# Last stage of an encoder step: the residual goes in with the first expert's result, the last expert's rows are added by 0/1 products

## What is computed

```python
lg = (xn @ w_router_group); grp = argmax(lg); top_v, top_i = top_k(le_sel, 2)
combine = sum(one_hot(eidx, 32) * wk[..., None], axis=1)
for e in range(32):
    h = silu(xn @ w_gate[e]) * (xn @ w_up[e])
    y = y + combine[:, e:e+1] * (h @ w_down[e])
x = x + y                                   # the residual
return rmsnorm(x, g_final), states, history
```

## Time and profile before

| | us |
|---|---|
| median of 3 runs | 883.58 (881.55 to 886.76) |
| the profiled execution, its own time | 883.38 |
| its span | 881.8 |
| PE busy | 792.7 (90%) |
| DVE / ACT / POOL busy | 257.7 / 118.8 / 128.3 |
| HBM read / written | 246.44 MB / 14.58 MB |

### The profile page before, as it was taken

One profiled execution on the slowest core, in us unless ns is written; L12 is line 12 of the kernel. 1 busy time (PEld: TensorE's weight loads), 2 busy tenths in 40 slices (PEclk: granted clock), 3 DMA queues, 4 the chain that ended last, 5 costly groups with the idle time before them and its releaser, 6 DMA issues.

```text
span 881.8 us, 9472 instructions
## 1 busy us (share of the span) xinstructions
PE 792.7 (90%) x3800; PEld 445.2 (50%) x3801; DVE 257.7 (29%) x730; ACT 118.8 (13%) x224; POOL 128.3 (15%) x224
## 2 busy tenths in 40 slices
PE   4999999999999999989999779779778877979876
PEld 4888888788888655533333323333223332323222
DVE  4799787100021355551111011111101111111115
ACT  5110021210100233301000000000000000000013
POOL 3000028900132200000111010000101000000000
PEclk9999999999999999999999998889899999989999
DMA  9657034062200492568999999999999999999966
GB/s 285 172 161 133 1 116 130 16 222 96 95 1 1 190 428 103 189 267 341 424 428 426 427 426 426 428 427 426 428 426 425 426 429 426 426 422 406 415 252 247
DMA packets 49056, 253.82 MB, mean 288 GB/s; under 512 B 17637, under 2 KB 18489, under 8 KB 36434
## 3 DMA queue, kind: packets, MB, share of 16 engines
q1 hardware_dynamic: 42050, 239.80, 68.1%
q0 software_dynamic: 6672, 12.86, 4.1%
q10 hardware_dynamic: 288, 0.53, 0.3%
HBM read 246.44 MB, written 14.58 MB: 296 GB/s over the span
## 4 chain that ended last, share of the span: by engine, by line
PE 63%; DMA 29%; SPq 4%; DVE 1%; issue 1%; ACT 1%; POOL 0%; POOLq 0%; ACTq 0%; DVEq 0%
PE ps L1436 26%; DMA arena<-in_w_exp_up 26%; PE ps L1688 14%; PE ps L1703 7%; PE ps L1561 6%; SPq L446 3%; PE ps L1775 2%; DMA x_rows<-arena 1%; PE ps L1500 1%; PE ps L1495 1%; DMA arena<-in_x_prompt 1%; PE ps L1678 1%; PE ps L1407 1%; PE ps L1695 1%; PE ps L1550 1%
## 5 line engine op out<-in xcount | busy, mean ns | idle before, releaser
L1688 PE MATMUL ps<-arena 128*64 128x512 f32 x1024 | 249.2, 641 | 59.2 <-DMA arena<-in_w_exp_up 58.7
L1436 PE MATMUL ps<-arena 128*128 128x272 f32 x992 | 229.6, 393 | 0.0
L1436 PEld LDWEIGHTS ps<-arena 128*128 128x128 f32 x992 | 188.1, 190 | 38.5
L1688 PEld LDWEIGHTS ps<-arena 128*64 128x64 f32 x1024 | 83.0, 148 | 203.2 <-issue 195.1
L1703 PE MATMUL ps<-arena 128*64 128x512 f32 x512 | 116.5, 595 | 2.0 <-DVE arena L1334 2.0
L1338 DVE TENSOR_SCALAR arena<-ps,arena 128x512 f32<-128x512 f32 x32 | 24.0, 751 | 201.3 <-PE ps L1703 201.3
L819 DVE TENSOR_TENSOR arena<-arena 128x256 f32<-128x256 f32 (+11 forms) x217 | 74.6, 344 | 13.3 <-ACT arena L728 4.0
L1703 PEld LDWEIGHTS ps<-arena 128*64 128x64 f32 x512 | 37.8, 137 | 65.0 <-issue 60.8
L1303 DVE TENSOR_TENSOR arena<-ps,arena 128x1024 f32<-128x1024 f32 x15 | 18.4, 1225 | 177.6 <-PE ps L1678 177.6
L588 POOL DMA_INDIRECT y_parts<-arena x32 | 32.0, 1000 | 239.9 <-DVE arena L1338 239.9
L769 ACT ACTIVATE arena<-ps,arena 128x512 f32<-128x512 f32 x32 | 22.0, 689 | 309.9 <-PE ps L1688 309.9
(11 more groups left out here) (224 smaller groups left out, 489.2 us busy)
## 6 DMA issues: line engine op xcount, KB each, us to landing
arena<-in_w_exp_gate SPq DMA_DIRECT2D x29, 2048.0 KB, 42.5
arena<-in_w_exp_up SPq DMA_DIRECT2D x29, 2048.0 KB, 32.2
arena<-in_w_exp_down SPq DMA_DIRECT2D x29, 2048.0 KB, 37.8
arena<-in_w_in SPq DMA_DIRECT2D x6, 2048.0 KB, 9.4
arena<-in_w_exp_gate SPq DMA_DIRECT2D x12, 512.0 KB, 13.2
arena<-in_w_exp_up SPq DMA_DIRECT2D x12, 512.0 KB, 18.8
arena<-in_w_exp_down SPq DMA_DIRECT2D x6, 1024.0 KB, 18.8
arena<-in_x_prompt SPq DMA_DIRECT2D x8, 512.0 KB, 6.4
```

Of the source, the lines that this page charges most:

```text
L1436: last = pe.matmul(dst[:, hh, 0:HALF], w[:, k, m * P:(m + 1) * P], rhs[:, k, hh * HALF:(hh + 1) * HALF], start=(k == 0), stop=(k == kk - 1))
L1688: last = pe.matmul(ps[n * TILE:(n + 1) * TILE, 2 + par, :], x_t[:, k, :], w[:, k, :], start=(k == 0), stop=(k == KD - 1))
```

## The change

- The residual is added with the first choice's result. DVE finds for each slot whether it is the token's first choice (`first`). ACT copies the x2 rows of a pair out of `xg`, times `first`, into `y_sb[0]` (even expert) and `x_odd` (odd expert): `fold_two`, four ACT instructions of 64x512 for a pair. `result` becomes a scalar_tensor_tensor that scales and adds.
- `xg` is still one buffer and now has a second reader, so `next_gather(j)` also waits for `folded >= 2 * j`. `fold_two(j)` stands on ACT behind the silu of expert 2j.
- `gu_rows` becomes one buffer (the other is `x_odd`), and the copy of gate and up waits for `gu_turned >= e`.
- The last expert's rows are not scattered. They are added by a product of `picks` (is this the slot's token, 0 or 1, 128 x 544, made by POOL's iota and one DVE instruction) with `y_sb[1]`. The reload of `y_parts` then waits for experts 0 to 30 alone.
- As the last expert's rows of `y_parts` are no longer written, all of `y_parts` (4.5 MB) is set to zero by 9 DMAs of POOL behind the first arrival of w_in.
- x2 is not reloaded. g_final comes as one row of 4 KB (`g_row`), and PE spreads it over the partitions with two products behind `turn_gate_up(30)`, where it waits for it.
- The last stage goes through the tiles in the order 0, 1, 2, 3, sample; the sample tile also goes through PE, with POOL adding its two parts, and DVE adds the parts of tiles 1 and 2. The mean and EPS move into the ACT instructions.

```diff
-END_ORDER = (4, 0, 1, 2, 3)
+LOAD_ORDER = (4, 0, 1, 2, 3)
+END_ORDER = (0, 1, 2, 3, 4)
...
-            sp.wait_ge(x2_stored, 16 * TT)
             sp.wait_ge(down_done, NE - 3)
-            sp.dma_start(ring[9]..., x2_rows[0:SEQ]...).then_inc(x2_back, 16)
-            sp.dma_start(x2_end[4][0:DEC], x2_rows[SEQ:NT]).then_inc(x2_back, 16)
-            sp.dma_start(g_end, a["g_final"]....to_broadcast((P, D))).then_inc(g_in, 16)
+            sp.dma_start(g_row, a["g_final"].rearrange("(o d) -> o d", o=1)).then_inc(g_in, 16)
...
             sp.wait_ge(y_all, 1)
-            for par in range(2):
-                sp.wait_ge(y_stored[par], 16 * NP)
+            sp.wait_ge(y_stored[0], 16 * NP)
+            sp.wait_ge(y_stored[1], 16 * (NP - 1))
...
+            pool.wait_ge(w_stream[0], 16)
+            by_part = y_parts.rearrange("(p n) c -> p (n c)", p=P)
+            for c in range(0, span, D):
+                pool.dma_start(by_part[:, c:c + w], zeros[:, 0:w]).then_inc(parts_zeroed, 16)
...
+            def next_gather(j):
+                pool.wait_ge(xt_done, j + 1)
+                pool.wait_ge(folded, 2 * j)
+                gather(j)
             gather(0)
-            pool.wait_ge(xt_done, 2)
-            gather(1)
+            next_gather(1)
             for e in range(NE):
-                j = e // 2 + 2
-                if e % 2 == 0 and j < NP:
-                    pool.wait_ge(xt_done, j + 1)
-                    gather(j)
+                if e >= 2 and e % 2 == 0 and e // 2 + 1 < NP:
+                    next_gather(e // 2 + 1)
+                if e == NE - 1:
+                    break
...
+            def fold(dst, rows, col, n):
+                for half in range(2):
+                    last = act.activation(dst[half * TILE:(half + 1) * TILE], xg[rows, half * F:(half + 1) * F],
+                                          ACT.Copy, scale=col[rows])
+                last.then_inc(folded, n)
+            def fold_two(j):
+                act.wait_ge(xg_in[j % 2], 16 * (j // 2 + 1))
+                if j:
+                    act.wait_ge(y_stored[0], 16 * j)
+                fold(y_sb[0], slice(0, TILE), first[:, 2 * j:2 * j + 1], 1)
+                if j:
+                    act.wait_ge(x_odd_free, j)
+                fold(x_odd, slice(TILE, P), first[:, 2 * j + 1:2 * j + 2], 1)
+            act.wait_ge(first_ready, 1)
+            fold_two(0)
...
                 gate(e % 2, e + 1)
+                if e and e % 2 == 0:
+                    fold_two(e // 2)
+                if e == NE - 2:
+                    act.wait_ge(g_spread, 1)
+                    act.activation(g_end..., ps[:, 0:2, :], ACT.Copy).then_inc(g_ready, 1)
...
-                dve.tensor_scalar(y_sb[par], ps[:, 6 + par, :], scale, None, ALU.mult).then_inc(y_ready, 1)
+                dve.wait_ge(folded, done)
+                last = dve.scalar_tensor_tensor(out=y_sb[par], in0=ps[:, 6 + par, :], scalar=scale, in1=residual,
+                                                op0=ALU.mult, op1=ALU.add)
...
+                if e == NE - 2:
+                    pe.wait_ge(g_in, 32)
+                    for half in range(2):
+                        last = pe.matmul(ps[:, half, :], ones[0:1, :], g_row[:, half * F:(half + 1) * F], start=True, stop=True)
+                    last.then_inc(g_spread, 1)
...
+            def pick(i, first, end):
+                for half in range(2):
+                    last = pe.matmul(ps[:r, 2 * (i % 4) + half, :], picks[rows, i * P:i * P + r], y_sb[1][rows, :],
+                                     start=first, stop=end)
+            pe.wait_ge(y_back[0], 16)
+            add(0, y_end[0][:, 0:D], True, False)
+            add(0, y_end[0][:, D:2 * D], False, False)
+            pe.wait_ge(y_ready, NE)
+            pick(0, False, True).then_inc(sum_done, 1)
+            for i in (1, 2):
+                pick(i, True, False)
+                pe.wait_ge(pair_sum, i)
+                add(i, y_end[i][:, 0:D], False, True).then_inc(sum_done, 1)
+            pick(3, True, False)
+            add(3, y_end[3][:, 0:D], False, False)
+            add(3, y_end[3][:, D:2 * D], False, True).then_inc(sum_done, 1)
+            pe.wait_ge(final_ready, 1)
+            pick(4, True, False)
+            pe.wait_ge(sample_sum, 1)
+            add(4, y_end[4][:, 0:D], False, True).then_inc(sum_done, 1)
```

More of the change, by code:

```diff
@@ L592, in put_entries @@
             def put_entries():
-                for par in range(2):
-                    pool.wait_ge(y_stored[par], 16 * NP)
+                pool.wait_ge(y_stored[0], 16 * NP)
+                pool.wait_ge(y_stored[1], 16 * (NP - 1))
+                pool.wait_ge(y_ready, NE)
                 pool.sem_inc(ov_done, 1)
@@ L774, in gate @@
                 act.activation(h[par], src[:, :, 0:TILE], ACT.Silu).then_inc(silu_ready, 1)
+            def fold(dst, rows, col, n):
+                for half in range(2):
+                    last = act.activation(dst[half * TILE:(half + 1) * TILE], xg[rows, half * F:(half + 1) * F], ACT.Copy,
+                                          scale=col[rows])
+                last.then_inc(folded, n)
[9 more added lines that the diff above has]
+            fold_two(0)
             act.wait_ge(slot_w_ready, 1)
             for e in range(NE):
-                if e >= 2:
-                    act.wait_ge(gu_turned, e - 1)
+                if e:
+                    act.wait_ge(gu_turned, e)
                 gate_up_out(e % 2, e + 1, slot_w[:, 1, e:e + 1])
@@ L787, in more @@
                 act.wait_ge(ov_idx, n)
+                act.wait_ge(ov_x, n * 16)
+                act.wait_ge(ov_first_ready, n)
+                fold(y_sb[0], slice(0, TILE), ov_first, 1)
                 gate_up_out(0, n + NE, ov_tab[:, 2:3])
@@ L1343, in _ @@
                     x_out(e // 2 + 3)
-                if e >= 2:
-                    dve.wait_ge(y_stored[e % 2], 16 * (e // 2))
-                result(e % 2, e + 1, slot_w[:, 0, e:e + 1])
+                if e == NE - 1:
+                    dve.wait_ge(token_no_ready, 1)
+                    dve.tensor_scalar(picks, token_no, last_token, None, ALU.is_equal).then_inc(picks_ready, 1)
+                if e >= 2 and e % 2:
+                    dve.wait_ge(y_stored[1], 16 * (e // 2))
+                result(e % 2, e + 1, slot_w[:, 0, e:e + 1], x_odd if e % 2 else y_sb[0])
+                if e % 2:
+                    dve.wait_ge(y_ready, e + 1)
+                    dve.sem_inc(x_odd_free, 1)
             def more(i, n):
@@ L1360, in _, with add_pair @@
             overflow(dve, more)
[L1362 to L1370, removed]
+            def add_pair(i):
+                dve.wait_ge(y_back[i], 16)
+                y_i = y_end[i][:ROWS[i]]
+                dve.tensor_tensor(y_i[:, 0:D], y_i[:, 0:D], y_i[:, D:2 * D], ALU.add).then_inc(pair_sum, 1)
@@ L1371, in _, with final @@
+            def final(n):
+                i = END_ORDER[n]
                 r = ROWS[i]
[L1372 to L1375, removed]
                 dve.wait_ge(root3, n + 1)
-                inverse_root(mean, root_i)
-                x_i, g_i = (x.rearrange("p (h n) -> p h n", h=2) for x in (x2_end[i][:r], g_end[:r]))
@@ new lines, in final @@
+                tt(root_i, root_i, tmp, ALU.mult)
+                y_i, g_i = (x.rearrange("p (h n) -> p h n", h=2) for x in (y_end[i][:r, 0:D], g_end[:r]))
+                dve.scalar_tensor_tensor(out=y_i, in0=ps[:r, 2 * (i % 4):2 * (i % 4) + 2, :], scalar=root_i,
+                                         in1=g_i, op0=ALU.mult, op1=ALU.mult).then_inc(final_ready, 1)
+            add_pair(1)
+            add_pair(2)
+            dve.wait_ge(g_ready, 1)
+            for n in range(TT):
+                final(n)
@@ L1768, in more @@
                 down(0, ring[2].rearrange("p (k n) -> p k n", k=4))
-            overflow(pe, more)
-            pe.wait_ge(x2_back, 32)
+            overflow(pe, more, last_result)
+            pe.wait_ge(y_all, 1)
+            pe.wait_ge(g_ready, 1)
             def add(i, part, first, end):
+                r = ROWS[i]
                 for half in range(2):
-                    last = pe.matmul(ps[:, 2 * i + half, :], ident, part[:, half * F:(half + 1) * F], start=first, stop=end)
-                return last
@@ L1778, in _ @@
[L1778 to L1785, removed]
+                    last = pe.matmul(ps[:r, 2 * (i % 4) + half, :], ident[:r, :r], part[:r, half * F:(half + 1) * F],
+                                     start=first, stop=end)
@@ new lines, in add @@
+                return last
+            def pick(i, first, end):
+                r = ROWS[i]
+                for half in range(2):
+                    rows = slice(half * TILE, (half + 1) * TILE)
+                    last = pe.matmul(ps[:r, 2 * (i % 4) + half, :], picks[rows, i * P:i * P + r], y_sb[1][rows, :],
+                                     start=first, stop=end)
+                return last
+            pe.wait_ge(y_back[0], 16)
```

(2 more changed lines are left out.)

80 lines of the change are left out of this document (54 added, 26 removed).

## The result

The changed kernel takes 934.13 us (median of 4 runs, 932.82 to 937.38), the kernel before in the same session 882.96: ratio 1.0584, 95% interval 1.0562 to 1.0605. It is 5.8% slower; 940 us were forecast, with a range of 905 to 965.

The account below looks back on a forecast made before the run. PE set the pace until about 480 us, then the weight stream, PE again at the end. With 14 gather stalls, expert 30's turn ends at 892.3; plus 45.7 gives span 938.0, so 940 us, range 905 to 965.

Parts of the forecast that it names:

- The gather decides: Expert part: the gather, now waiting for fold_two, makes PE stall at turn_x for pairs 2 to 15, +59.6 us.
- T30: End of expert 30's turn of gate and up on PE: forecast at 892.3 instead of 832.72.
- The chain of a stall: Even expert's turn to turn_x: silu 0.49, folds 2.3, POOL start 0.8, gather landing 11.7, together 15.3 us.
- The clock: PE behind each stall: a lowered clock makes turn and down product 1.8 us longer, bounds 0 and 2.6.
- P: Time of one pair of experts when stalled: 15.3 + 16.48 + 1.8 = 33.6 us.
- The stream not binding: Expert part: a pair's 33.6 us exceeds the weight stream's 31.20, so loads wait for free slots, not PE for weights.
- rival 1: Gather lands before PE needs it; PE waits for g_row behind expert 30's turn: 895 us, chance 0.06.
- g_row: Before the last stage: issued behind expert 28's down product, the row lands before PE needs it, so no wait.
- The start: Zeroing 4.5 MB, 11 us of the DMA engines, fits into their free room: 0 us, bounds 0 and +3.
- The end: From expert 30's turn to the end of the span: 45.7 us instead of 49.05, a gain of 3.4.
- Rival 2: Neither the gather nor g_row makes PE wait: 880 us, -0.4%, chance 0.04.
- Rival 3: Scatters slowed beyond 10.7 us by gathers on one queue delay the folds too: 965 us at 12.5, chance 0.04.

Follow-up runs that it names:

- the run with the wait alone and gather first: Kernel before, only the next gather moved: asked for behind the even expert's silu, ahead of the odd expert's scatter; no folds: 898.16 us, ratio 1.0165.
- the run with the gather freed: Changed kernel, but the folds copy a constant, leaving out the residual, and the gather waits for the turn alone: 893.08 us, ratio 1.0092.
- the run without any wait: Changed kernel with folds from a constant, the gather waiting for the turn alone, and g_row loaded by ACT's queue at expert 29: 878.0 us, ratio 0.9935.

## Why the prediction was right, step by step

- **The gather decides, and 14 times.** Right, and shown: freeing it takes 41 us off at once, and 56 with the row that lay below it. T30 was forecast at 892.3 and is 893.15. The forecast of 940 lies 5.9 above the median of 934.13: 3.05 of it is the end, and most of the rest is that this execution lies 3.2 above the median, where the forecast has the median 0.2 above it.
- **The chain of a stall.** 15.3 behind the turn was forecast. The first stall has it, but out of two errors that cancel, and the eleven behind it have 14.5 to 14.9: the four folds are 2.9 and not 2.3 (0.72 each; the nearest row, 0.63 with the sum, was low for 64 partitions, and the 0.55 from PSUM too), so they end 3.3 behind the turn and not 2.8; the landing is 11.12 in that chain, 10.6 in the median, not 11.7. The surcharge of 1.0 for the scatter ahead on the queue is not there at 3.2 us of distance: 10.6 against 10.7 before, where the scatter was 8 us ahead. At 1.3 us it is real, 1.9 (12.2 against 10.3).
- **The clock.** 1.8 forecast; 2.6 measured in the first stall, the upper bound, and up to 3.0 behind it. That what follows was a turn and a down product, not wide first products, was no reason to take less. The run with PE kept busy shows the cause: behind the same waits, filled, `turn_x` and the down product take 1.1 and 3.6.
- **P.** 33.6 forecast; 34.08 over the first twelve stalls: the shorter chain and the dearer clock nearly cancel. It is less at the last two (idle of 5.24 and 4.42), where experts 29 to 31 load in pieces and the gathers land in 8.1 and 7.2 us; why sooner was not tested. Over all 14, (893.15 - 421.94) / 14 = 33.66. That the mean is within 0.1 of the forecast is partly luck.
- **The stream not binding.** Right: no idle in front of the first products. The remark in the first paragraph, that there is room only for delays that begin once the lead is gone, is too strict, as the run with the wait alone and gather first shows. No term was built on it, and rival 1 has the right measure, a mean of 29.3.
- **g_row.** In the changed kernel it binds nothing, as forecast. Rival 1 was the second layer: its 895 is the 893 of the run with the gather freed. The Trainium skill's rule that a DMA of one row, not split, runs on one engine (DMA: Bandwidth & Descriptors, "Why a DMA increments its semaphore by 16 and not by 1") would have allowed an early landing. The two packets of the row on ACT's queue agree with the rule, but on SP's queue it took 16.0 us behind the weights, against 18.3 for the median of the last down pieces. Being small and on few engines saved it hardly anything; another queue did.
- **The start.** The zeros fill the room that was there: in 33 to 44 us the DMA share is 0.98 and not 0.33, the small load still ends DVE's wait at 19.62, and the first turn of gathered rows is at 386.23, 0.05 earlier. 0 was right.
- **The end.** 45.7 forecast, 42.65 measured. The mis-sized term is the products of the last stage: 20.7 forecast, 17.95 measured. (14.02 / 16 is 0.876 and not 0.86, so by its own row the forecast should have been 21.0.) The adds, 28 records in 12.9 us, are 0.9 above their price of 14 x 0.86 = 12.0. The picks, 20 records in 5.0 us, are far below their 8.6:

```profile
915.32 1.99 PE L1861 MATMUL ps<-arena 64*128 64x512 f32 x8
```

Eight records of two picks take 1.92 us in the chain, a pick of four records 1.0 and not 1.72. The two halves of a pick use 64 partitions each, and their records overlap: a record lasts 0.59 by itself, as one of the adds does, but they follow each other at 0.24 to 0.27 and not at 0.45 to 0.48. The row to price them by was not L1775 but the first products, 32 records of 128x64 in 7.02 us, 0.22 for a record of half the array. The Trainium skill says it too (TensorEngine Tiling (Array Packing), "Tiling Modes"): tiles of half the array work independently of each other. This trace agrees, with its 0.24 for a record. From the last scaled row to the end of the span are 2.4 us and not 2.8. The last stage is thus worth 6.4 us and not 3.4.
- **The rivals.** Rival 2's 880 is the 878 of the run without any wait. Rival 3 did not occur: the 64 folds of ACT have 7.6 us of idle in front of them in all, 6.8 of it for the first gather, so none waited for a scatter.

## What to carry to other kernels

- When a new reader is given to a buffer, work out the loop that refills it: from the reader's end over the queue and the landing to the next use. Here a reader that is done 3.3 us behind the turn of gate and up, on an engine that was 8% busy in that stretch, cost 60 us, as the refill takes 11 us and had 7 left before the folds even began.
- How much a consumer of a stream may lose is set by its mean over all rounds, and a stream that starts with a lead asks for more than its own pace: with eleven slots loaded ahead the mean that costs nothing was 29.3 us a pair, not 31.2. A loop of 30.3 was no slower than the stream and still lost 11.7 us.
- Look under the first wait for the next. The row of g_final cost nothing in the changed kernel and 15 us as soon as the gather was freed. And a small load does not belong behind a full queue if another queue is empty.

## What the runs showed of the hardware that I had not expected

- How close two indirect DMAs stand on POOL's queue counts: a gather 1.3 us behind a scatter lands in 12.2 (median), 3.2 us behind in 10.6, 8 us behind in 10.7, and ahead of it in 10.3 to 10.5, all with the weights streaming. The first one, with a DMA share of 0.25, landed in 4.1.
- With the weights streaming (DMA share 1.02), a row of 4 KB on ACT's queue was through within 3.9 us of its issue; on SP's queue, which carried the weights, it took 16.0.
- An idle of 7.5 to 8.3 us costs PE 2.6 us more in the turn and the down product behind it, no less than the 2.0 to 2.5 that an idle of 5 us cost the wide first products. An idle of 5.39 in the run with the wait alone and gather first makes the turn and the down product as slow (1.97 and 5.24). Sixteen useless records in each idle gave back 31.4 us in all.
- ACT's copy of 64x512 from SBUF, scaled by a column, takes 0.72, more than the 0.63 of 128x512 with a sum.
